# Stops of a diffusion-transformer kernel: where the modulation products stand, and who scales, shifts and splits the normed tokens

## The reference

```python
def rmsnorm(x, g):
    xf = x.astype(jnp.float32)
    y = xf * lax.rsqrt(jnp.mean(xf * xf, axis=-1, keepdims=True) + RMS_EPS)
    return (y * g.astype(jnp.float32)).astype(x.dtype)

def modulate(h, shift, scale):
    return h * (1 + scale) + shift
...
for l in range(DEPTH):
    mod_x = (jax.nn.silu(c) @ w_ada[l] + b_ada[l])[:, None, :]
    mod_c = jax.nn.silu(c_ctx) @ w_ada[l] + b_ada[l]
    sh1, sc1, gt1, sh2, sc2, gt2 = jnp.split(mod_x, 6, axis=-1)
    hx = modulate(rmsnorm(x, g_pre_mix[l]), sh1, sc1)
    ...
    x = x + gt1 * rmsnorm(y_x, g_post_mix[l])
    hx = modulate(rmsnorm(x, g_pre_ffn[l]), sh2, sc2)
    x = x + gt2 * rmsnorm(channel_mixer(hx, l, ...), g_post_ffn[l])
    # the context tokens likewise, with c_ctx's modulation
```

## Time and profile before

| | before |
|---|---|
| median of 3 timed runs | 2254.86 us (2254.19 to 2255.01) |
| the profiled execution's own time | 2250.69 us |
| its span, first to last instruction | 2248.9 us |
| TensorE busy | 2183.3 us, 97% of the span |
| VectorE busy | 768.3 us, 34% |
| ScalarE busy | 555.4 us, 25% |
| mean granted TensorE clock | 0.986 |

### The profile page before, as it was taken

One profiled execution on the slowest core, in us unless ns is written; L12 is line 12 of the kernel. 1 busy time (PEld: TensorE's weight loads), 2 busy tenths in 40 slices (PEclk: granted clock), 3 DMA queues, 4 the chain that ended last, 5 costly groups with the idle time before them and its releaser, 6 DMA issues.

```text
span 2248.9 us, 54675 instructions
## 1 busy us (share of the span) xinstructions
PE 2183.3 (97%) x24222; PEld 1624.1 (72%) x24222; DVE 768.3 (34%) x1563; ACT 555.4 (25%) x1080; POOL 48.9 (2%) x63
## 2 busy tenths in 40 slices
PE   7999999999999999988999999999999999999999
PEld 4777877778688888868898998566666666666666
DVE  4465255444644233356737752000001010101012
ACT  4245344323422222334535440000000000000001
POOL 0000000000020000000001000000000000000000
PEclk8999999999999999989999999999999999999999
DMA  6323223335483223433234488999999999999993
GB/s 256 131 113 132 85 113 128 117 122 204 171 274 111 97 101 134 162 134 113 97 113 139 154 328 319 416 405 417 409 412 408 414 407 410 412 408 411 419 408 160
DMA packets 88535, 548.91 MB, mean 244 GB/s; under 512 B 10592, under 2 KB 16480, under 8 KB 28288
## 3 DMA queue, kind: packets, MB, share of 16 engines
q1 hardware_dynamic: 55232, 352.68, 40.5%
q10 hardware_dynamic: 28912, 178.14, 19.7%
q0 software_dynamic: 4176, 14.81, 2.0%
HBM read 529.08 MB, written 16.52 MB: 243 GB/s over the span
## 4 chain that ended last, share of the span: by engine, by line
PE 84%; DVE 8%; DMA 3%; ACT 3%; issue 2%; ACTq 0%; SPq 0%; DVEq 0%
PE S L1911 15%; PE O L1911 13%; PE pp L1535 9%; PE pp L1537 9%; PE pp L1536 9%; PE T L1911 8%; DVE wsp L1029 2%; PE S L1535 2%; PE S L1536 2%; PE T L1536 2%; PE S L1537 2%; PE T L1537 2%; PE T L1535 2%; PE T L1725 1%; DMA slabs<-in_w_moe 1%
## 5 line engine op out<-in xcount | busy, mean ns | idle before, releaser
L1911 PE MATMUL S<-slabs,M 128*32 128x256 f32 x7168 | 482.2, 379 | 0.5 <-DMA slabs<-in_w_moe 0.4
L1029 DVE TENSOR_TENSOR wsp<-raw,wsp 128x1024 fp32r<-128x1024 f32 (+3 forms) x248 | 263.9, 1085 | 313.5 <-ACT wsp L668 307.2
L1911 PEld LDWEIGHTS S<-slabs,M 128*32 128x32 f32 x7168 | 248.5, 110 | 144.6 <-issue 2.2
L1535 PE MATMUL pp<-hx,wsp 128*128 128x512 f32 (+1 forms) x800 | 285.1, 356 | 21.2 <-DVE M L1273 4.7
L1911 PE MATMUL T<-slabs,M 128*32 128x256 f32 x3584 | 292.9, 379 | 0.9 <-issue 0.8
L1911 PE MATMUL O<-slabs,M 128*32 128x256 f32 x5376 | 291.5, 379 | 0.0
L1485 DVE TENSOR_TENSOR M<-M,S 128x256 f32<-128x256 f32 x56 | 23.6, 422 | 755.9 <-ACT M L979 755.9
L1536 PE MATMUL pp<-hx,wsp 128*128 128x512 f32 (+1 forms) x800 | 277.4, 347 | 0.0
L1537 PE MATMUL pp<-hx,wsp 128*128 128x512 f32 (+1 forms) x800 | 277.2, 347 | 0.0
L1911 PEld LDWEIGHTS O<-slabs,M 128*32 128x32 f32 x5376 | 174.7, 110 | 115.4
L668 ACT ACTIVATE wsp<-raw 128x1024 fp32r<-128x1024 f32 (+3 forms) x248 | 226.8, 938 | 107.7 <-PE T L1537 77.4
(11 more groups left out here) (255 smaller groups left out, 2234.8 us busy)
## 6 DMA issues: line engine op xcount, KB each, us to landing
slabs<-in_w_moe SPq DMA_DIRECT2D x175, 1024.0 KB, 16.1
slabs<-in_w_moe ACTq DMA_DIRECT2D x161, 1024.0 KB, 16.6
raw<-in_w_main SPq DMA_DIRECT2D x84, 1024.0 KB, 5.0
M<-in_w_main SPq DMA_DIRECT2D x25, 1024.0 KB, 9.6
slabs<-in_w_main SPq DMA_DIRECT2D x15, 1024.0 KB, 8.6
raw<-in_w_br SPq DMA_DIRECT2D x24, 512.0 KB, 3.7
xm<-in_w_main SPq DMA_DIRECT2D x8, 1024.0 KB, 5.2
raw<-in_w_dn SPq DMA_DIRECT2D x8, 768.0 KB, 4.1
```

What stands on the lines that cost most here:

```text
L1029: dve.tensor_tensor(wsp[:, slot, 1, 0:w], raw[:, rslot, half * w:half * w + w], wsp[:, slot, 0, 0:w], ALU.subtract).then_inc(lo_done, 1)
L1535: mm(dst, w_hi, x_hi, start=first, stop=False)
L1911: ins = mm(banks[g // 2][32 * c:32 * c + 32, 256 * (g % 2):256 * (g % 2) + 256], x(k, g), slab_e[i % RAW_E][:, 1024 * k + 256 * c:1024 * k ...
```

## The change

It has two parts, both at n = 2 and n = 4 alone.

1. `stop` on TensorE: products 1 to 6 stand ahead of the sum of the first pair (before: 1 to 3), 7 ahead of the second (4 and 5), 8 ahead of the third (6 and 7), 9 ahead of the spreading of the root (8), 10 behind it (9 and 10), and then five matmuls that compute nothing needed (`keep_up(5)`).
2. `prenorm`: VectorE's scale step is one product of `xm` and `R` for all 512 tokens, into one of three buffers `gt3` (before: two of `gt`). ScalarE applies scale and shift in place (two instructions, each with a scale and a bias column). The high part of odd tiles is written by ScalarE, that of even tiles by VectorE, each for 512 tokens at once; the low part is one VectorE subtraction. The orders are the lists `SPLIT_ORDER` (VectorE) and `SHIFT_ORDER` (ScalarE).

```diff
--- before.py
+++ after.py
@@ -139,6 +139,10 @@
 ADA_BESIDE_A = 8
 PLANS = [mixer_plan(ADA_MIXER), mixer_plan([])]
 DN_STAGE = KT
+SHIFT_ORDER = [("shift", 0)] + [p for k in range(1, KT, 2)
+                                for p in [("shift", k)] + [("shift", k + 1)] * (k + 1 < KT) + [("cast", k)]]
+SPLIT_ORDER = [("scale", 0), ("scale", 1), ("cast", 0), ("lo", 0)] + [
+    p for k in range(2, KT, 2) for p in (("scale", k), ("scale", k + 1), ("lo", k - 1), ("cast", k), ("lo", k))] + [("lo", KT - 1)]
 
 
 def spread(steps, slots):
@@ -287,6 +291,7 @@
         row_copied, cols_done, mod_ready = sem("row_copied"), sem("cols_done"), sem("mod_ready")
         sq_done, sum_done, sd_done = sem("sq_done"), sem("sum_done"), sem("sd_done")
         sq_added, pair_added = sem("sq_added"), sem("pair_added")
+        hi_cast = sem("hi_cast")
         gate_ready, y_gated = sem("gate_ready"), sem("y_gated")
         dg_done, cast_done = sem("dg_done"), sem("cast_done")
         scaled, affine, h_split = sem("scaled"), sem("affine"), sem("h_split")
@@ -762,17 +767,36 @@
                     act.activation(dst, gt[:, k % 2, c], ACT.Identity, bias=mod[:, l, 3 * which, k, s:s + 1]
                                    ).then_inc(affine, 1)
 
+            shifted = [2 * KT]
+
+            def shift_step(n, l, which, k):
+
+                act.wait_ge(scaled, 8 * (n // 2) + k + 1)
+                for s in range(2):
+                    v = gt3[:, k % 3, SEQ * s:SEQ * s + SEQ]
+                    act.activation(v, v, ACT.Identity, bias=mod[:, l, 3 * which, k, s:s + 1], scale=am[:, 2 * which, k, s:s + 1]
+                                   ).then_inc(affine, 1)
+
             def prenorm(n, l, which, N, hcount):
                 for k in range(KT):
                     act.wait_ge(x_upd, 8 * hcount[0] + k + 1)
                     square(xm[:, :, k, :] if N == TOK else xm[:, 0, k, :], n, k, N)
                 norm_root(n, N)
                 act.wait_ge(mod_ready, (1, 2, 3, 4)[n // 2])
-                for k in range(KT):
-                    affine_step(n, l, which, N, k)
-                    if n < 6 and k == 1:
-                        act.wait_ge(tile_done, t_stop[n // 4] + ADA_STOP)
-                        act.activation(adr_f[:, 0, :], O[0][:, 0:256], ACT.Copy).then_inc(stop_rows, 1)
+                if n < 6:
+                    for what, k in SHIFT_ORDER:
+                        if what == "shift":
+                            shift_step(n, l, which, k)
+                        else:
+                            act.wait_ge(affine, shifted[0] + 2 * (k + 1))
+                            act.activation(hx[:, 0, k, :], gt3[:, k % 3, :], ACT.Copy).then_inc(hi_cast, 1)
+                        if k == 1 and what == "cast":
+                            act.wait_ge(tile_done, t_stop[n // 4] + ADA_STOP)
+                            act.activation(adr_f[:, 0, :], O[0][:, 0:256], ACT.Copy).then_inc(stop_rows, 1)
+                    shifted[0] += 2 * KT
+                else:
+                    for k in range(KT):
+                        affine_step(n, l, which, N, k)
                 use_table((None, ACT.Silu, ACT.Exp, ACT.Exp)[n // 2])
 
             def load_bias(l, head):
@@ -1156,11 +1180,24 @@
 
             def prenorm(n, l, which, N):
                 token_roots(n, N)
-                for k in range(KT + 1):
-                    if k < KT:
+                if n < 6:
+                    for what, k in SPLIT_ORDER:
+                        v = gt3[:, k % 3, :]
+                        if what == "scale":
+                            if k >= 3:
+                                dve.wait_ge(h_split, 8 * (n // 2) + k - 2)
+                            dve.tensor_tensor(v.rearrange("p (a b) -> p a b", b=SEQ), xm[:, :, k, :],
+                                              R[:, :].rearrange("p (a b) -> p a b", b=SEQ), ALU.mult).then_inc(scaled, 1)
+                        elif what == "cast":
+                            dve.wait_ge(affine, aff[0] + 2 * (k + 1))
+                            own.link(dve.tensor_copy(hx[:, 0, k, :], v))
+                        else:
+                            if k % 2:
+                                dve.wait_ge(hi_cast, 4 * (n // 2 - 1) + k // 2 + 1)
+                            dve.tensor_tensor(hx[:, 1, k, :], v, hx[:, 0, k, :], ALU.subtract).then_inc(h_split, 1)
+                else:
+                    for k in range(KT):
                         scale_step(n, which, N, k)
-                    if k >= 1 and n < 6:
-                        lo_step(n, l, which, N, k - 1)
                 aff[0] += KT * (N // SEQ)
 
             aff = [0]
@@ -1610,17 +1647,17 @@
 
             def stop(b, n):
 
-                for j, products in enumerate(((1, 2, 3), (4, 5), (6, 7))):
+                for j, products in enumerate(((1, 2, 3, 4, 5, 6), (7,), (8,))):
                     for p in products:
                         stop_product(b, p)
                     pe.wait_ge(pair_added, 3 * b + j + 1)
                     token_sums(sq4[:, (2 * j + 1) % 4, :], TOK, j == 0, False).then_inc(sum_done, 2)
                 norm_sum(n, 6, TOK)
                 norm_sum(n, 7, TOK)
-                stop_product(b, 8)
+                stop_product(b, 9)
                 norm_cast(n, TOK)
-                stop_product(b, 9)
                 stop_product(b, 10)
+                keep_up(5)
 
             def ada_product(dst, w):
```

## The result

| | before | after |
|---|---|---|
| median, 12 runs each on the same chips | 2252.86 us | 2257.73 us |
| lowest and highest | 2245.17, 2256.94 | 2253.01, 2261.94 |
| ratio, 95% interval | | 1.0028 [1.0017, 1.0039] |
| the profiled execution's own span | 2248.9 us | 2251.2 us |

The change made the kernel 5 to 6 us slower (4.9 by the medians, 6.3 by the ratio). The twelve runs of before differ by up to 12 us, far more than its first three (0.8 us), so a single profile is one draw, and the intervals decide. The reason for the spread turned out to be part of the answer: where TensorE's clock falls differs from run to run, and the runs with a lower mean clock are the longer ones (shown at the end of the experiments).

A forecast was written before the change was run, and what follows sets the result against it. TensorE, holding 84% of the chain that ended last, was taken to bound the kernel. Stops +1.1 and -3.4, loops +1.5 and +2.2 sum to +1.4 us: 2256.3 from the median 2254.86, range 2250.5 to 2262.

The forecast's parts named there:

- Both terms of the clock: The forecasts for TensorE's two stops, which depend on its clock: +1.1 us at the first, -3.4 at the second.
- 2261 and one fall of 1.7: Slower case: first stop +5.8, second -3.4, loops +3.7 give 2261; a clock fall in one loop adds up to 1.7 us.
- Ring of 4.10 us a round: `prenorm` loop: VectorE and ScalarE wait on each other in turn, so two tiles take 4.10 us against 3.54.
- First loop +1.5: First norm: TensorE resumes 18.9 us after the spreading of the root, against 17.38, so 1.5 us later.
- Second +2.2: Second norm's loop: TensorE's end of `first_pair` counts, 18.5 us after the spreading against 16.3, so 2.2 us later.
- The estimate of 0.09 for a second column: Loop: a second per-partition column adds 0.09 us to each ScalarE shift instruction, making a pair 1.10.
- `keep_up(5)` at no cost: Behind the spreading: product 10 and the five idle matmuls take 2.2 us, before the first low part at 3.0.
- The order of events in the first stop: First stop: products 5 to 8 wait for slabs landing one by one, with sums between; spreading ends at 600.8 at full clock.
- +1.1, which I take: First stop: two sums and two products at half clock cost 3.6 us more, about 1.2 hidden in slab waits; net +1.1.
- the second rival: Slower, chance 0.25: clock falls among first-stop products 5 to 8 and stays low through the sums, +5.8 us there, +6.1 total.
- -3.4, the value that I take: Second stop: shorter waits, with only product 9 and the spreading at half clock, end it at 994.3 against 997.67.
- the worse bound: Second stop: with the clock at half from the second sum on, the gain is only about 0.6 us.

The follow-up runs named there:

- the loop alone: The changed kernel with the old order of the stops back, so only the new `prenorm` loop differs from the kernel before: 1.0011 [0.9998, 1.0024].
- the cast early: New `prenorm` loop with the old stops, and ScalarE's cast of an odd tile right behind its shift, against the kernel before: 0.9983 [0.9973, 0.9994].
- stops kept: The kernel before with the new order at both stops, the old loop, and more idle matmuls in both stops: 0.9999 [0.9986, 1.0013].
- best: Changed loop, odd-tile cast right behind its shift; old order at first stop, new at second; idle matmuls in waits and last sums; against before: 0.9964.

## Why the prediction was right or wrong, step by step

The time, 2257.7 us, is inside the range, 1.4 above the value. The side is not what the forecast held likeliest: 0.63 went to no difference, 0.25 to slower. Against the kernel before, +1.4 us was forecast and +4.9 (medians) to +6.3 (ratio) measured. That the time came so close is partly luck: the value was counted from 2254.86, the median of three runs, and the median of twelve is 2.0 lower; from there the same sum gives 2254.3, and the measured time is 3.5 above it. Both terms of the clock were too low, by 2.4 and 2.5 us. The upper end of the range is 0.7 short of its own words: 2261 and one fall of 1.7 are 2262.7, not 2262.

- **The loop: right.** Ring of 4.10 us a round: measured 4.04. First loop +1.5: +1.5. Second +2.2: +2.0. The estimate of 0.09 for a second column: 0.088. That VectorE's work falls and the loop still gets longer is shown both ways, by the loop alone and by the cast early.
- **`keep_up(5)` at no cost: right.** It takes 1.38 us (L1594) ahead of a low part that comes later; TensorE waits another 0.94 for this in the first norm.
- **The order of events in the first stop: right, its price wrong.** The slabs made the products wait at 587.0, 589.5, 592.0 and 594.5. The step "+1.1, which I take" failed: it let the clock fall for two sums and two products, with part hidden in waits. What fell was the end: product 8, the three last sums, product 9 and the spreading, where nothing waits and nothing hides it. Measured +3.5 in the profile of after; 23.2 to 25.9 us in the four kernels that have this order without extra idle matmuls, against 19.1 to 23.0 in those with the old one. This is the second rival's mechanism, here at three fifths of its +5.8; at 25.9 us it was all of it (+6.2).
- **The second stop: "-3.4, the value that I take" failed, in both of its ends.** The work ahead of the last sums came out as told. The last sums then ran at half (5.28 us, not 2.84), which I had as the worse bound (-0.6; measured -0.9). And the 21.67 us subtracted from was one draw of a wide spread: in four other kernels that left this stop alone it took 17.7 to 18.2 us three times and 23.0 once. With the new order and no other idle matmuls it is 19.7 to 21.5. The gain that the shorter waits should give is not there on average: 1.0000 for this edit by itself.
- **The rule of the Trainium skill** (page "TensorE: Matmul & The Clock Gate", section "HAM oscillation — how this bites in real kernels") spoke against the change, and the runs agree with it for the first stop: short bursts between waits for DMA, then a stretch of 10 us at 0.51. The agreement has limits. The DMA waits in the section's example are longer than any here (at most 1.5 us); and at the second stop, where no product waits for DMA, the last sums ran at 0.52 as well. The sums keep TensorE busy on paper, and the clock fell in them or stayed low; that they, and not the waits ahead of them, let it fall is not shown.
- **Chances.** I had weighed the terms' middles, each as if it were independent and could as well be lucky. The clock's terms are not symmetric: a fall is followed by sums that run at half and last twice as long.

Open: why the clock falls in one run of a stop and not in the next of the same code. The traces show where it fell, not why there. How far the two stops' losses hang together is known only to the width of the intervals (1.0024 as a sum, 1.0014 together).

## What to carry to other kernels

Where two engines hand tiles back and forth, follow the ring of waits before adding up busy times: putting a cast one place later on an engine that is mostly idle cost 1.1 us a tile pair (4.04 against 2.91), more than the 0.6 (3.54 to 2.9) that the new split of the work was to save. In these stops TensorE's clock was lost behind short waits and in the thin matmuls at the end; idle matmuls in the waits and between the sums turned a loss of 0.24% into a gain of 0.14% (the new order at the first stop, 1.0024 without them and 0.9986 with them) though they lengthen the stage on paper. They did not hold the clock every time (stops kept, best). And when terms hang on the clock, read the same stretch in several executions before pricing a gain against one.

## What the runs showed of the hardware

- TensorE at 100% busy can be at half clock: 24 rows of 128 x 1 sums took 2.84 us in some executions and 5.28 in others of the same code.
- Where the clock falls differs from run to run, and with it the time: 2242.4 to 2258.1 us over 32 runs of the kernel before on one chip, 0.7%, with mean clocks from 0.984 to 0.989, for differences of 0.1 to 0.3% that were to be told apart.
- ScalarE's activation of 128x256 took 0.382 us with no per-partition column, 0.474 to 0.502 with one and 0.590 with two, each the mean of a group, of three different lines.
